# State space: GpSimd's waits on itself, projections in eighths, one output bank, four banks for the gated unit, idle products

## The chip, the cores and the metric

The kernel runs on one core of a Trainium2 chip, as one launch. The time is device time of that core in microseconds. Before the change it is 1918.82 us, the median of 3 runs (1918.71 to 1918.95). All arithmetic is in float32.

## The reference

Four transformer-like layers run over 256 tokens of width 1024: two layers of attention with a long convolution, an even layer (two kinds of attention, then a dense feed-forward), and an odd layer: a diagonal state space mixer, then a mixture of 8 experts, 2 per token. The change lies in the odd layer's mixer and in the router behind it, with one line ahead of the mixer's norm.

```python
def s5_mixer(h, w_in, lam_re, lam_im, log_dt, b_re, b_im, c_re, c_im, d_skip, w_glu, w_o):
    ...
    u = h @ w_in
    ug = u.reshape(B, S, S5_GROUPS, S5_GROUP)
    ...
    bu_re = jnp.einsum('sbgk,gpk->sbgp', ut, bb_re)
    bu_im = jnp.einsum('sbgk,gpk->sbgp', ut, bb_im)
    ...
    _, _, xr, xi = lax.associative_scan(combine, (ar_t, ai_t, bu_re, bu_im), axis=0)
    y = jnp.einsum('sbgp,gkp->bsgk', xr, c_re) - jnp.einsum('sbgp,gkp->bsgk', xi, c_im)
    y = y.reshape(B, S, D_MODEL) + d_skip * u
    y = jax.nn.gelu(y)
    y = y * jax.nn.sigmoid(y @ w_glu)
    return y @ w_o

def moe_swiglu(h, w_router, w_gate, w_up, w_down):
    logits = (h @ w_router).astype(jnp.float32)
    top_val, top_idx = lax.top_k(logits, TOP_K)
    weights = jax.nn.softmax(top_val, axis=-1)
    ...
```

There are 64 groups of 16 channels with 64 complex states each. The recurrence of a state over 256 tokens is computed as a rotation, a real scan with a decay, and a rotation back.

## The kernel before, in words

Every engine has a program of its own, written out by hand, and they meet through semaphores. TensorE writes to eight PSUM banks of 128 x 512 numbers. A float32 product is two matrix instructions in the trace.

**Projection.** `s5_in(c, j, part)` computes u = h @ w_in, transposed, in four chunks c of two blocks j of 128 channels. A part is four of the eight products that one block takes; the chunks use bank 2 and bank 3 in turn. ScalarE's `s5_in(c)` (L1554) copies a chunk to `uT` and counts `free`. Six parts run ahead of the state space (all of chunk 0 and half of chunk 1), the other ten one per round, by `IN_AT`.

**State tiles.** A state tile i (of 32) holds 128 states, those of two groups. Work goes in rounds p of two tiles:
- TensorE's `s5_state(p)` (L1103) multiplies `uT` by the input matrices into banks 4 and 5 or 0 and 1. It waits until VectorE is done with the pair of two rounds ago.
- VectorE rotates (L2243 to L2246) and scans (L2250, L2251) a tile, with each operation waiting for the one before, and counts `z5_ready`. The scan's result `zz` has two buffers, so tile i waits for `cz_ready` of tile i - 2.
- GpSimd rotates back: two products of 128 x 256 into `cz` (L2444), a difference (L2446) and a sum (L2447) into `xs`, which has four buffers. `link` makes GpSimd wait for each operation before it issues the next. It counts `cz_ready` once per tile.
- TensorE's `s5_out(o)` (L1119, L1122, L1126) multiplies the states of tiles o and o + 1 by the output matrices, two rounds behind the state products. Four tiles fill one output tile y in bank 6 or 7, in turn.
- VectorE's `y_tile(j)` (L2233) adds d_skip * u to an output tile, in program order behind state tile 4j + 6; ScalarE's `s5_gelu(j)` (L1559) follows.

**Gated unit.** `s5_glu(k, half)` (L1083) multiplies output tile k by four of the eight column blocks of w_glu, so 8 matrix instructions. The first half (banks 2 and 3) goes into rounds 10 to 15, the second (banks 4 and 5) into rounds 16 and 17, by `GLU_AT`. Round 17 holds eight such calls behind the last outputs. ScalarE then takes the sigmoid of a bank (L1571), VectorE multiplies (L2261), and TensorE multiplies by w_o (L1148).

**Weights.** SyncE requests six blocks of 2 MB into `wmix` (L444): blocks 0 and 1 for the projection, 2 and 3 for the gated unit once chunks 1 and 3 are projected (`grp_ps`), 4 and 5 for w_o behind tiles 8 and 24 (`cz_ready`). The experts' first weights are requested when the gated unit ends and when the output projection ends.

**Router.** Behind the norm, TensorE computes the logits (L1158, 16 products of 8 columns), waits for VectorE's choice of experts (`rt_step`), computes ranks (L1164 to L1168), waits for VectorE (`oh_ready`), gathers the first expert's tokens (L1029), loads the number of work items into a register, and starts the experts (L932, L950).

## Time and profile before

| | us |
|---|---|
| median of 3 runs | 1918.82 |
| the profiled execution | 1918.2 |
| its span | 1916.4 |
| TensorE busy | 1862.4 (97%) |
| VectorE busy | 644.5 (34%) |
| ScalarE busy | 357.7 (19%) |
| GpSimd busy | 113.3 (6%) |

The shares are averages over stages with different limits. The state space is the stretch from 1005 to 1122 us of the span, the output projection follows until 1149, norm and router until 1173, and the experts take the rest. Times in the rows below are us from the start of the span. A row of a timeline merges instructions of one line that follow each other: start, time until the last one's end, engine, line, operation, buffers, shapes and count. In brackets stands how long the engine was idle ahead of it, and what ended that.

### The profile page before, as it was taken

Reading aid. Unit: us, or ns where it says so; the run is one execution under the profiler, and the core shown is the slowest. Engines: PE = TensorE matmul, PEld = TensorE weight load, DVE = VectorE, ACT = ScalarE, POOL = GpSimd, SP = SyncE. Lnnn points to the kernel's source line nnn. Section 1 sums busy time; section 2 is a strip of 40 time slices with the busy share of each in tenths; the row PEclk is TensorE's granted clock in tenths of the full one; section 3 lists DMA queues with packets and bytes.
Section 4 is the critical chain, followed back from the end, with each engine's and each line's share of the span. In section 5 each row is a group of like instructions: output and inputs, shape, how many; then the busy total and the mean of one; then the engine's idle time right before and its main releaser. Section 6 shows DMA issues by size and latency. Waiting matters only on the chain.

```text
span 1916.4 us, 28949 instructions
## 1 busy us (share of the span) xinstructions
PE 1862.4 (97%) x12112; PEld 1040.3 (54%) x12112; DVE 644.5 (34%) x1479; ACT 357.7 (19%) x779; POOL 113.3 (6%) x166
## 2 busy tenths in 40 slices
PE   8999999999999999999998898999999999999998
PEld 6577866678775765867767664232323333333332
DVE  3464414354513484352357824010101010110102
ACT  3322103322103132233221012010101010101001
POOL 0000000000000000000006800000000000000000
PEclk9999999999999999999999998999999999999999
DMA  8345675254665314634421337999999999999993
GB/s 350 116 183 201 238 302 228 88 220 176 243 269 227 132 45 155 263 132 181 171 88 45 133 132 302 399 401 380 390 388 385 395 385 391 387 392 361 418 376 136
DMA packets 45529, 488.87 MB, mean 255 GB/s; under 512 B 5285, under 2 KB 6949, under 8 KB 11945
## 3 DMA queue, kind: packets, MB, share of 16 engines
q1 hardware_dynamic: 39136, 471.73, 61.6%
q10 hardware_dynamic: 5160, 11.82, 1.6%
q0 software_dynamic: 1152, 4.19, 0.6%
q8 instruction: 57, 0.93, 0.2%
q14 instruction: 24, 0.19, 0.0%
HBM read 481.82 MB, written 12.20 MB: 258 GB/s over the span
## 4 chain that ended last, share of the span: by engine, by line
PE 89%; DVE 4%; POOL 3%; issue 1%; ACT 1%; ACTq 1%; DMA 0%; DVEq 0%; POOLq 0%
PE bank L950 21%; PE bank L590 15%; PE bank L980 12%; PE bank L902 8%; PE bank L914 4%; PE bank L748 3%; PE bank L582 3%; PE bank L754 3%; PE bank L575 3%; POOL arena L2444 2%; PE bank L603 2%; PE bank L1148 1%; PE bank L571 1%; PE bank L964 1%; PE bank L1083 1%
## 5 line engine op out<-in xcount | busy, mean ns | idle before, releaser
L950 PE MATMUL bank<-arena 128*32 128x512 f32 x4096 | 457.5, 592 | 1.1 <-issue 1.1
L590 PE MATMUL bank<-arena 128*128 128x256 f32 x1408 | 313.3, 382 | 0.0
L950 PEld LDWEIGHTS bank<-arena 128*32 128x32 f32 x4096 | 136.7, 110 | 301.5 <-issue 301.5
L590 PEld LDWEIGHTS bank<-arena 128*128 128x128 f32 x1408 | 265.6, 191 | 53.0 <-issue 14.6
L980 PE MATMUL bank<-arena 128*32 128x512 f32 x2112 | 238.2, 595 | 0.0
L2195 DVE TENSOR_TENSOR arena<-arena,bank 128x256 f32<-128x256 f32 x64 | 27.0, 421 | 568.0 <-ACT arena L1521 517.8
L902 PE MATMUL bank<-arena 128*128 128x256 f32 x704 | 153.8, 379 | 0.1
L902 PEld LDWEIGHTS bank<-arena 128*128 128x128 f32 x704 | 133.2, 190 | 19.9 <-issue 2.1
L980 PEld LDWEIGHTS bank<-arena 128*32 128x32 f32 x2112 | 62.9, 109 | 133.8 <-issue 133.8
L1521 ACT ACTIVATE arena<-bank 128x256 f32<-128x256 f32 x64 | 24.6, 384 | 519.4 <-PE bank L950 519.3
L914 PE MATMUL bank<-arena 128*128 128x512 f32 x176 | 77.2, 592 | 0.0
L2444 POOL TENSOR_TENSOR arena<-arena 128x256 f32<-128x256 f32 x64 | 46.5, 727 | 258.0 <-DVE arena L2251 253.1
L575 PE MATMUL bank<-arena 128*128 128x512 f32 x128 | 55.4, 593 | 1.8 <-ACT arena L1215 1.8
L748 PE MATMUL bank<-arena 128*128 128x256 f32 x256 | 57.0, 381 | 0.0
L754 PE MATMUL bank<-arena 128*128 128x512 f32 x128 | 56.4, 596 | 0.2 <-DVE arena L2045 0.2
L582 PE MATMUL bank<-arena 128*128 128x256 f32 x256 | 56.3, 381 | 0.0
L914 PEld LDWEIGHTS bank<-arena 128*128 128x128 f32 x176 | 33.4, 190 | 37.8 <-issue 37.3
L582 PEld LDWEIGHTS bank<-arena 128*128 128x128 f32 x256 | 48.3, 190 | 9.8 <-issue 3.4
L748 PEld LDWEIGHTS bank<-arena 128*128 128x128 f32 x256 | 48.2, 190 | 7.5 <-issue 0.8
L2163 DVE TENSOR_TENSOR arena<-arena,bank 128x256 f32<-128x256 f32 x22 | 9.2, 421 | 125.4 <-ACT arena L1494 125.4
L2432 POOL TENSOR_TENSOR arena<-arena 128x512 f32<-128x512 f32 x22 | 28.1, 1279 | 363.9 <-ACT arena L1215 363.8
L603 PE MATMUL bank<-arena 128*32 128x512 f32 x384 | 45.8, 598 | 0.0
(472 smaller groups left out, 1741.5 us busy)
## 6 DMA issues: line engine op xcount, KB each, us to landing
arena<-in_wgu SPq DMA_DIRECT2D x88, 2048.0 KB, 10.8
arena<-in_w SPq DMA_DIRECT2D x46, 2048.0 KB, 8.2
arena<-in_wdn SPq DMA_DIRECT2D x88, 1024.0 KB, 11.1
arena<-in_modw SPq DMA_DIRECT2D x24, 2048.0 KB, 9.7
arena<-in_wf SPq DMA_DIRECT2D x11, 3072.0 KB, 10.2
arena<-slot_rows ACTq DMA_DIRECT2D x7, 384.0 KB, 11.3
arena<-in_flt_deltas ACTq DMA_DIRECT2D x2, 1024.0 KB, 11.6
slot_rows<-arena ACTq DMA_DIRECT2D x7, 192.0 KB, 6.3
```

Of the source, the lines that this page charges most:

```text
L575: ins = mm(bank[b][:, :], mT[:, k, h * P:(h + 1) * P], w[:, k * 512:(k + 1) * 512], start=(k == 0), stop=(k == KT - 1))
L582: ins = mm(bank[b][:, j * S:(j + 1) * S], w[:, col:col + P], y_in[:, k, :], start=(k == 0), stop=(k == 3))
L590: ins = mm(bank[b][:, j * S:(j + 1) * S], w[:, col:col + P], hT[:, k, :], start=(k == 0), stop=(k == KT - 1))
L603: ins = mm(bank[n % 2][r, :], band[:, k, 31 - c:63 - c], ring[at % RING][:, k * 512:(k + 1) * 512], start=(k < 4), stop=(k >= 4), skip_gro ...
L748: ins = mm(bank[n % 2][:, j * S:(j + 1) * S], w[:, col:col + P], hT[:, k, :], start=(k == 0), stop=(k == KT - 1))
L754: ins = mm(bank[n % 2][:, :], lhs(k), w[:, k * 512:(k + 1) * 512], start=(k == 0), stop=(k == KT - 1))
L902: ins = mm(bank[4 + f][:, u * S:(u + 1) * S], w[:, col:col + P], hT[:, k, :], start=(k == 0), stop=(k == KT - 1))
L914: ins = mm(bank[2 * t + i][:, :], hid[:, d % 2, f, t * P:t * P + P], w[:, col:col + 512], start=(d == 0 and f == 0), stop=(d == FFC - 1 an ...
L950: ins = mm(bank[w % 2][32 * j:32 * j + 32, :], hTe[:, k, TOK * b:TOK * b + TOK], wslot[SLOT[c]][:, k, :], start=(k == 0), stop=(k == KT - ...
L980: return mm(bank[4 + n][32 * g:32 * g + 32, :], lhs, dslot[c % RING][:, f, n * 512:(n + 1) * 512], start=first, stop=last, skip_group_chec ...
L2432: ins = pool.tensor_tensor(modsum, modsum, modout[:, n % 2, :], ALU.add)
L2444: link(pool.tensor_tensor(cz[:, n], zz[:, o % 2], tab[o][:, n, :].unsqueeze(1).broadcast_to([P, 2, PAIRS]), ALU.mult))
```

## The change

- **GpSimd:** within a tile only the difference waits, for both products (`link.mark` counts without waiting). `cz` has two buffers. `cz_ready` counts twice per tile, and every wait on it is doubled.
- **Projection:** a unit is two products (an eighth of a block pair's 16). Only chunk 0 runs ahead of the state space, the other 24 units go by `IN_STEPS` into rounds 0 to 10. All chunks use bank 2, so a chunk's first unit waits for ScalarE's copy of the chunk before.
- **Outputs:** all output tiles use bank 6. VectorE's `y_tile(j)` moves ahead by one state tile, and `s5_out` of a new output tile waits for it.
- **Gated unit:** `s5_glu(k, c)` does two of the eight column blocks (4 matrix instructions); the four groups have banks 3, 7, 2 and 5. Three of them go on during the state space.
- **ScalarE:** its first three gelus are issued between the copies.
- **Idle products:** `keep_warm(n, b)` multiplies the identity by 512 columns of constants into bank b, n times, and nobody reads it: one ahead of the norm before the mixer, two behind the logits, one ahead of the gather, three behind it.

On GpSimd, this is a state tile from the middle, before:

```order
L2444 TENSOR_TENSOR arena<-arena 128x256 [waits sy_ps,z5_ready,cz_ready]
L2444 TENSOR_TENSOR arena<-arena 128x256 [waits pool_chain]
L2446 TENSOR_TENSOR arena<-arena 128x128 [waits pool_chain]
L2447 TENSOR_TENSOR arena<-arena 128x128 [waits pool_chain]
L2444 TENSOR_TENSOR arena<-arena 128x256 [waits sy_ps,z5_ready,cz_ready]
L2444 TENSOR_TENSOR arena<-arena 128x256 [waits pool_chain]
```

And after, where L2471, L2473 and L2474 are the same operations:

```order
L2471 TENSOR_TENSOR arena<-arena 128x256 [waits cz_ready,sy_ps,z5_ready]
L2471 TENSOR_TENSOR arena<-arena 128x256
L2473 TENSOR_TENSOR arena<-arena 128x128 [waits pool_chain]
L2474 TENSOR_TENSOR arena<-arena 128x128
L2471 TENSOR_TENSOR arena<-arena 128x256 [waits cz_ready,sy_ps,z5_ready]
L2471 TENSOR_TENSOR arena<-arena 128x256
```

Two of the three waits inside a tile are gone. The wait for `cz_ready` that opens a tile asked for the tile just before, and now asks for the tile two back.

On TensorE, at the start of the state space, before (L1066 projection, L1103 state products; the first row is the rest of the products ahead of the loop):

```order
L1066 MATMUL bank<-arena 128x256 x16
L1103 MATMUL bank<-arena 128x128 [waits even_free]
L1103 MATMUL bank<-arena 128x128 x7
L1066 MATMUL bank<-arena 128x256 x4
L1103 MATMUL bank<-arena 128x128 x8
L1066 MATMUL bank<-arena 128x256 x4
```

And after (L1084 projection, L1122 state products):

```order
L1084 MATMUL bank<-arena 128x256 x8
L1122 MATMUL bank<-arena 128x128 [waits even_free]
L1122 MATMUL bank<-arena 128x128 x7
L1084 MATMUL bank<-arena 128x256 [waits even_free]
L1084 MATMUL bank<-arena 128x256 x5
L1122 MATMUL bank<-arena 128x128 x8
L1084 MATMUL bank<-arena 128x256 x6
```

Eight products moved from ahead of the first state products to behind them.

On TensorE, in the router, after (L1177 logits, L738 the idle products, L1184 to L1188 ranks, L1042 gather, L394 the register load); before, the rows are the same without those of L738:

```order
L1177 MATMUL bank<-ev,arena 128x8 x8
L738 MATMUL bank<-cst 128x512 x2
L1184 MATMUL bank<-arena,cst 128x8 [waits rt_step]
L1185 MATMUL bank<-arena,cst 128x8
L1186 MATMUL bank<-arena,cst 128x8
L1187 MATMUL bank<-arena,cst 128x8
L1188 MATMUL bank<-arena,cst 128x8
L738 MATMUL bank<-cst 128x512
L1042 MATMUL bank<-arena 128x96 [waits oh_ready,gb_ready]
L1042 MATMUL bank<-arena 128x96 x15
L738 MATMUL bank<-cst 128x512 x3
L394 TENSOR_LOAD itab [waits items_ready,hta_ready]
```

Each idle product stands ahead of a wait in TensorE's queue, and none waits itself.

```diff
--- before.py
+++ after.py
-IN_AT = {n: (1 + (n + 2) // 4, (n + 2) // 2 % 2, n % 2) for n in range(10)}
-GLU_AT = {**{10 + k: [(k, 0)] for k in range(6)}, 16: [(0, 1), (1, 1)], 17: [(6, 0), (2, 1), (3, 1), (4, 1), (7, 0), (5, 1), (6, 1), (7, 1)]}
+IN_UNITS = [(c, j, u) for c in range(1, 4) for j in range(2) for u in range(4)]
+IN_STEPS = [3, 3, 2, 3, 3, 1, 2, 1, 2, 1, 3]
+GLU_AT = {5: [(0, 0), (0, 1)], 7: [(1, 0), (1, 1)], 9: [(2, 0), (2, 1)], 11: [(3, 0), (3, 1)], 12: [(0, 2), (1, 2), (2, 2)],
+          13: [(4, 0), (4, 1)], 14: [(3, 2), (4, 2)], 15: [(5, 0), (5, 1)], 16: [(5, 2), (0, 3), (1, 3)],
+          17: [(6, 0), (6, 1), (6, 2)] + [(k, 3) for k in range(2, 7)] + [(7, c) for c in range(4)]}
+GLU_BANK = (3, 7, 2, 5)
...
-        cz = view(CH * 3 + 2048, 2, 2, PAIRS)
+        cz = [view(CH * 3 + at, 2, 2, PAIRS) for at in (2048, 512)]
...
-                    sp.wait_ge(sm["cz_ready"], (8, 24)[n - 4])
+                    sp.wait_ge(sm["cz_ready"], (16, 48)[n - 4])
...
+            def keep_warm(n, b):
+                for _ in range(n):
+                    mm(bank[b][:, :], ident, cst[:, 0:512], start=True, stop=True)
...
             gate_rows(3, gdiag5)
+            keep_warm(1, 4)
             norm(4, (0, 1, 4, 5))
-            def s5_in(c, j, part):
-                if j + part == 0 and c % 2 == 0:
-                    pe.wait_ge(landeds[c // 2], 16)
+            def s5_in(c, j, unit):
+                if j + unit == 0:
+                    if c % 2 == 0:
+                        pe.wait_ge(landeds[c // 2], 16)
+                    if c:
+                        n = G3 + c - 1
+                        pe.wait_ge(free[n % 2], n // 2 + 1)
                 w = wmix[c // 2]
-                for k in range(4 * part, 4 * part + 4):
+                for k in range(2 * unit, 2 * unit + 2):
...
-                    ins = mm(bank[2 + c % 2][:, j * S:(j + 1) * S], w[:, col:col + P], hT[:, k, :],
+                    ins = mm(bank[2][:, j * S:(j + 1) * S], w[:, col:col + P], hT[:, k, :],
...
-            def s5_glu(k, half):
+            def s5_glu(k, c):
                 if k == 0:
-                    if half:
+                    if c == 2:
+                        pe.wait_ge(free[(G3 + 3) % 2], (G3 + 3) // 2 + 1)
+                    elif c == 3:
                         pe.wait_ge(sm["z5_ready"], STATE_TILES - 2)
...
                 pe.wait_ge(sm["gelu_ready"], k + 1)
-                for o in range(4 * half, 4 * half + 4):
+                for o in (2 * c, 2 * c + 1):
...
-            for c, j, part in ((0, 0, 0), (0, 0, 1), (0, 1, 0), (0, 1, 1), (1, 0, 0), (1, 0, 1)):
-                s5_in(c, j, part)
+            for j in range(2):
+                for u in range(4):
+                    s5_in(0, j, u)
...
-                pe.wait_ge(sm["cz_ready"], o + 2)
-                if o % 4 == 0 and o >= 8:
-                    pe.wait_ge(sm["y_out"], j - 1)
+                pe.wait_ge(sm["cz_ready"], 2 * (o + 2))
+                if o % 4 == 0 and o:
+                    pe.wait_ge(sm["y_out"], j)
...
-                y = bank[6 + j % 2]
+                y = bank[6]
...
-                if p in IN_AT:
-                    s5_in(*IN_AT[p])
-                for k, half in GLU_AT.get(p, []):
-                    s5_glu(k, half)
+                for unit in IN_UNITS[sum(IN_STEPS[:p]):sum(IN_STEPS[:p + 1])]:
+                    s5_in(*unit)
+                for k, c in GLU_AT.get(p, []):
+                    s5_glu(k, c)
...
+            keep_warm(2, 3)
             pe.wait_ge(sm["rt_step"], 1)
...
+            keep_warm(1, 3)
             pe.wait_ge(sm["gb_ready"], 4)
             gather()
+            keep_warm(3, 3)
             pe.wait_ge(sm["hta_ready"], 28)
...
             s5_in(0)
             s5_in(1)
+            s5_gelu(0)
             s5_in(2)
-            s5_gelu(0)
+            s5_gelu(1)
+            s5_gelu(2)
             s5_in(3)
-            for j in range(1, 8):
+            for j in range(3, 8):
                 s5_gelu(j)
...
-                        dve.wait_ge(sm["cz_ready"], i - 1)
+                        dve.wait_ge(sm["cz_ready"], 2 * (i - 1))
...
-                if i >= 6 and i % 4 == 2:
+                if i >= 5 and i % 4 == 1:
                     y_tile(i // 4 - 1)
...
+                if o >= 2:
+                    pool.wait_ge(sm["cz_ready"], 2 * o - 2)
+                t = cz[o % 2]
                 for n in range(2):
-                    link(pool.tensor_tensor(cz[:, n], zz[:, o % 2],
-                                            tab[o][:, n, :].unsqueeze(1).broadcast_to([P, 2, PAIRS]), ALU.mult))
-                link(pool.tensor_tensor(xs[o % 4][:, 0, :], cz[:, 0, 0, :], cz[:, 1, 1, :], ALU.subtract))
-                pool.tensor_tensor(xs[o % 4][:, 1, :], cz[:, 0, 1, :], cz[:, 1, 0, :], ALU.add).then_inc(sm["cz_ready"], 1)
-                pool.wait_ge(sm["cz_ready"], o + 1)
+                    (link if n else link.mark)(pool.tensor_tensor(t[:, n], zz[:, o % 2],
+                                                                  tab[o][:, n, :].unsqueeze(1).broadcast_to([P, 2, PAIRS]), ALU.mult))
+                pool.tensor_tensor(xs[o % 4][:, 0, :], t[:, 0, 0, :], t[:, 1, 1, :], ALU.subtract).then_inc(sm["cz_ready"], 1)
+                pool.tensor_tensor(xs[o % 4][:, 1, :], t[:, 0, 1, :], t[:, 1, 0, :], ALU.add).then_inc(sm["cz_ready"], 1)
```

## Rows read from the trace of the kernel before

**Rows 1.** the chain that ended last, 995 to 1210 us, shares by line

```profile
by line: POOL arena L2444 18.5%; PE bank L950 12.9%; PE bank L1148 12.8%; PE bank L1083 8.8%; PE bank L1066 6.3%; POOL arena L2447 6.0%; POOL arena L2446 5.7%; issue 4.5%; PE bank L1029 2.9%; PE bank L980 2.1%; PE bank L1158 1.6%; PE bank L
```

**Rows 2.** groups of instructions on GpSimd; count, busy us, mean ns, idle before

```profile
L2444 POOL TENSOR_TENSOR arena<-arena 128x256 f32<-128x256 f32 x64 | 46.5, 727 | 258.0 <-DVE arena L2251 253.1
...
L2446 POOL TENSOR_TENSOR arena<-arena 128x128 f32<-128x128 f32 x32 | 14.5, 454 | 2.5
```

**Rows 3.** timeline, GpSimd, first and last state tile; start us, us

```profile
1019.34 1.54 POOL L2444 TENSOR_TENSOR arena<-arena 128x256 f32<-128x256 f32 x2 [253.07 <-DVE arena L2251]
...
1102.27 1.53 POOL L2444 TENSOR_TENSOR arena<-arena 128x256 f32<-128x256 f32 x2
```

**Rows 4.** timeline, VectorE, first operation of state tiles 0, 1, 6 and 7

```profile
1016.79 0.42 DVE L2243 TENSOR_TENSOR arena<-bank,arena 128x256 f32<-128x256 f32 x1 [10.62 <-PE bank L1103]
...
1019.29 0.42 DVE L2243 TENSOR_TENSOR arena<-bank,arena 128x256 f32<-128x256 f32 x1
...
1031.74 0.42 DVE L2243 TENSOR_TENSOR arena<-bank,arena 128x256 f32<-128x256 f32 x1
...
1034.63 0.42 DVE L2243 TENSOR_TENSOR arena<-bank,arena 128x256 f32<-128x256 f32 x1
```

**Rows 5.** timeline, TensorE, round 10 and the start of round 11

```profile
1065.40 1.18 PE L1103 MATMUL bank<-arena 32*128 32x128 f32 x16
...
1067.48 0.41 PE L1119 MATMUL bank<-arena 32*32 32x128 f32 x4 [0.91 <-POOL arena L2447]
...
1070.74 1.18 PE L1103 MATMUL bank<-arena 32*128 32x128 f32 x16
```

**Rows 6.** timeline, TensorE, from round 16 on

```profile
1101.20 5.07 PE L1083 MATMUL bank<-arena 128*128 128x256 f32 x16
...
1106.21 0.41 PE L1119 MATMUL bank<-arena 32*32 32x128 f32 x4
...
1107.55 14.08 PE L1083 MATMUL bank<-arena 128*128 128x256 f32 x64
```

**Rows 7.** timeline, start of the state space: first copy, first state products

```profile
1012.15 0.60 ACT L1554 ACTIVATE arena<-bank 128x512 f32<-128x512 f32 x1 [4.61 <-PE bank L1066]
...
1015.49 1.18 PE L1103 MATMUL bank<-arena 32*128 32x128 f32 x16
```

**Rows 8.** timeline, GpSimd, two memsets at the start

```profile
0.28 0.12 POOL L2605 MEMSET const-bfloat16-1.0<- 128x1 bf16 x1
...
0.31 0.12 POOL L2605 MEMSET const-uint8-127<- 128x1 uint8 x1
```

**Rows 9.** transfers into wmix, 990 to 1100 us, time to landing

```profile
DMA to landing us min/median/max: 7.8/8.0/12.7
```

**Rows 10.** timeline, TensorE, gate rows and the transposes of the next norm

```profile
998.48 1.88 PE L734 MATMUL bank<-arena,cst 128*128 128x512 f32 x4
...
1002.16 1.09 PE L519 MATMUL bank<-cst,arena 128*128 128x128 f32 x8 [1.80 <-DVE arena L1611]
```

**Rows 11.** windows: us, busy (count) of PE, PEld, DVE, ACT, POOL, clock, DMA share, GB/s

```profile
1161.00:1165.00 4.00, 2.65 (x13) 2.58 (x13) 2.38 (x11) 0.00 (x0) 0.00 (x0) 0.50 1.01 428
...
1200.00:1300.00 100.00, 99.71 (x906) 30.81 (x898) 10.82 (x23) 9.81 (x22) 0.00 (x0) 1.00 0.98 395
```

**Rows 12.** timeline, norm and router

```profile
1151.76 1.97 PE L519 MATMUL bank<-cst,arena 128*128 128x128 f32 x16 [0.85 <-DVE arena L1611]
...
1153.71 3.98 PE L1158 MATMUL bank<-ev,arena 128*128 128x8 f32 x32
...
1159.85 0.60 PE L1164 MATMUL bank<-arena,cst 128*128 128x8 f32 x2 [2.17 <-DVE arena L2359]
...
1162.27 0.18 DVE L2368 SCALAR_TENSOR_TENSOR arena<-bank,arena 128x16 f32<-128x16 f32 x1 [2.07 <-PE bank L1168]
...
1163.51 6.32 PE L1029 MATMUL bank<-arena 128*128 128x96 f32 x32 [1.35 <-DVE arena L2281]
...
1172.69 3.37 PE L932 MATMUL bank<-arena 128*32 128x512 f32 x16 [2.86 <-issue]
```

19 lines of the change are left out of this document (10 added, 9 removed).

## The prediction

> **What bounds the kernel now.** I read the chain that ended last first. Between 995 and 1210 us it lies mostly on GpSimd: L2444, L2446 and L2447 hold 30% of that stretch [rows 1]. Next I read GpSimd's groups: four operations per state tile, two of 727 ns and two of 454 ns (L2447 like L2446), 2.36 us of work [rows 2]. The timeline gives the cadence: tile 0 starts at 1019.34 and tile 31 at 1102.27, so 2.675 us per tile [rows 3]. The difference, 0.314 us, is four gaps of 0.078 us, one ahead of each operation, because each waits for the one before it. So GpSimd is never starved, and the state space costs 32 of its periods.
>
> VectorE is the next limit. One of its tiles takes 2.49 us (1019.29 to 1031.74 is five), and 2.89 us where an output tile is added, which makes 0.40 us for that [rows 4]. Four tiles cost it 4 x 2.49 + 0.40 = 10.36 us, against GpSimd's 10.70.
>
> TensorE comes third. From one pair of tiles to the next it has 5.34 us, of which it waits 0.91 us for GpSimd [rows 5]. After GpSimd's last tile, however, TensorE alone has the path: output products, 64 instructions of the gated unit, and then L1148 [rows 6].
>
> **Part 1: the start.** Before, 48 projection instructions run ahead of the first state products, though the first chunk of 32 is enough for them. ScalarE copies that chunk at 1012.15 in 0.60 us, while the state products start only at 1015.49 [rows 7]. After, TensorE stops at the chunk and waits for the copy: 1012.15 + 0.60 + 0.10 for the hand-over = 1012.85. Gain 2.64 us; VectorE's first tile moves from 1016.79 [rows 4] to 1014.15. The idle time of TensorE ahead of the copy, some 0.8 us, is already in this sum. The second chunk now comes in 3 + 3 + 2 units between pairs. It is wanted in round 4, so nothing waits for it.
>
> **Part 2: the loop.** Three of GpSimd's four waits on itself go (only the subtraction keeps one). Operations of GpSimd that do not wait are shown once, the memsets at the start: of 0.12 us each, they start 0.03 us apart, so they overlap by 0.09 us [rows 8]. Bounds of the new cadence, then: 2.675 us if the gaps are not due to the waits; 2.36 + 0.078 = 2.44 if they close; 2.675 - 3 x (0.078 + 0.09) = 2.17 if the operations also overlap. I take 2.44, the sum of the tensor rows themselves. The choice hardly matters, because VectorE at 10.36 per four tiles is slower than 9.76 and takes over the pace. VectorE runs 32 x 2.49 + 7 x 0.40 = 82.5 us, so its last scan ends at 1014.15 + 82.5 = 1096.65, and GpSimd's last tile 0.09 + 2.44 later, at 1099.2. Before it was 1102.27 + 2.59 = 1104.86. That is 5.7 us earlier: 2.6 from the start, 3.1 from the loop.
>
> On the pages: the Trainium skill, GPSIMD Engine Reference, section 2.1 (Instruction dispatch), says that a Pool instruction does not hold the next one back, and that each of its cores goes on as soon as its own share is done. The memsets agree with it [rows 8]. By that rule the 2.17 would stand; the sum stays the same.
>
> Is the cover there? Between pairs TensorE has 4.43 us of work with 8 instructions of projection or gated unit (5.34 - 0.91). One instruction of these costs 14.08 / 64 = 0.22 us [rows 5, 6]. The new tables put 2 or 3 units of 4 instructions into each round, 36 over rounds 3 to 16, 2.57 on average: 4.43 + 0.57 x 0.88 = 4.93 us, under VectorE's 5.18 per pair. A round with three units takes 5.31, over it by 0.13; state products are made a pair ahead, so this is absorbed.
>
> The output tiles now share one bank, and VectorE adds tile j - 1 one state tile earlier, behind state tile 4j + 1. TensorE's last outputs for it wait for GpSimd's tile 4j - 1, which with GpSimd in step ends 2.5 us after VectorE starts state tile 4j, and take 1.4 (L1119 to the last L1126), so they end at 3.9; the addition comes at 2 x 2.49 = 4.98. It has 1.1 us to spare. TensorE wants the bank again 2.4 us after the addition. Neither waits. The one projection bank costs a wait for a ScalarE copy (0.6 plus two hand-overs) in round 6, which has two units only. On SyncE, the weights of units (k, 2) are requested when the projections end, in round 10, and are wanted about 7.6 us later; such a transfer lands after 7.8 to 12.7 us [rows 9], the longest being the second of two issued together. The weights for the output projection, queued behind it, are not wanted before the loop ends. This is 0.2 us late if it lands like the fastest, 5 if like the slowest. I take 0.2, since it is the first of its two, and state products a pair ahead hide some 2 us.
>
> **Part 3: behind the loop.** Before, the last output products started at 1106.21, not at 1104.9, because 16 gated-unit instructions took 5.07 us (0.32 each instead of 0.22) [rows 6]. After, round 16 holds 12 instructions, 2.6 us at full clock and 4 at the slower pace. They start behind outputs at about 1094.2 + 1.34, so they end at 1098.2 to 1099.7. I take the later: 0.5 us late instead of 1.35, a gain of 0.8. Behind the last outputs there stood 64 instructions, now 48 (12 units of 4): 16 x 0.22 = 3.5 us less. The sigmoids of the first three groups end before the last unit does, as the last four units are one per group, 0.88 us apart, and a sigmoid takes no longer than the 0.60 of the copy of that shape in [rows 7]. Parts 1 to 3 sum to 2.6 + 3.1 + 0.8 + 3.5 = 10.0 us.
>
> **Part 4: idle products.** One is two instructions; the four at L734 take 1.88 us, so a product costs 0.86 to 0.94 at full clock [rows 10]. The one ahead of the norm ends near 1001.2, and TensorE waited 1.80 us there, until 1002.16: cost and gain nothing. It is hidden by VectorE's norm; without that cover it would cost its 0.9.
>
> At the router the clock had fallen to 1.2 GHz (granted 0.50) [rows 11] behind an idle time of 2.17 us. There ten small instructions run from 1159.85 until VectorE answers at 1162.27, and then 32 gather instructions take 6.32 us [rows 12]. The same small kind cost 3.98 / 32 = 0.124 each just before, and transposes of 128 columns 1.97 / 16 = 0.123. Warm, the ten take 1.3 instead of 2.3 us (gain 1.0) and the gather 32 x 0.123 = 3.9 instead of 6.3 (gain 2.4). The two products in the 2.17 us end before the wait does, the one ahead of the gather lies beside 1.24 us of VectorE. The three behind the gather take 2.6 to 2.8 us, where 2.86 passed anyway before the experts' first products. These three are what can cost: if the register load for the loop begins only behind them, up to 1.1 us is lost. Those first products, 16 in 3.37 us, would take 1.7 warm, by half (gain 1.65). Together 3.9 to 5.1; I take 3.9. Behind it TensorE is busy 99.7 of 100 us [rows 11] and every weight load waits for it, so the shift is kept.
>
> **Sum.** 10.0 + 3.9 = 13.9 us. The profiled execution took 1918.2 (span 1916.4), 0.6 under the median; from it 1904.3, from the median 1904.9. Small waits of the fuller TensorE are likelier than further gains, so I say 1905.2.
>
> **Rivals.**
> (a) GpSimd's gaps are no waits on itself: cadence 2.675 remains and the loop's 3.1 is not had. 1918.8 - 10.8 = 1908.0. The even 0.078 gaps behind every dependent step speak for it, the memsets against. Chance 0.12.
> (b) The clock is not held at the router: products at half speed last 3.5 us and overrun their 2.17 by 1.3, one before the gather as much again. The gather turns warm somewhere, the experts' first products are warm. Router gain 0.3 instead of 3.9: 1908.7. For it: the clock fell soon after the small products, so they may have weighed little. Chance 0.18.
> (c) TensorE becomes the bound: its reserve is 0.25 us per pair by my sum, and every wait for a copy, for weights or for the shared output bank eats from it. With all 16 pairs at 5.31 the loop loses 2.1, with a full late transfer 3 more: 1907.3 to 1910. Chance 0.17. The Trainium skill, Perfetto Trace Analysis, section Matmul Optimizations, asks for all eight PSUM banks to be in use; the change takes banks from projection and outputs. The trace of before has no wait for such a bank, so no run here yet shows the rule at work.
> (d) Slower: VectorE and GpSimd, now closer packed, slow each other in SBUF. From 0.43 us more per VectorE tile (17%) the gain is gone (32 x 0.43 = 13.8); with a quarter more on its 2.3 us busy, 0.57, it ends at 1904.9 + 18.2 = 1923. Against it: VectorE's first tile, with GpSimd idle, took 2.50 us, the later ones 2.49 [rows 4]. Chance 0.03.
> Forecast itself: 0.50.
>
> **Range.** The cases (a) to (c) reach from 1907 to 1910, all warm with overlap to 1902.5. So 1902 to 1910.5. What a measurement of this kernel can tell from no change is 0.2%, 3.8 us: faster means under 1915.0. All but (d), and mixtures of (a), (b) and (c) that go further than priced, lie there: faster 0.93, within 0.04, slower 0.03.
>
> **What would show it.** First state products at 1012.9 and VectorE's first tile at 1014.2; GpSimd's tiles spaced 2.49 with 2.89 once in four, and waiting for VectorE; its last one ending at 1099; 48 gated-unit instructions behind the last outputs in 10.5 us; L1148's successor at 1111.5. At the router granted clock 1.00, gather 3.9 us. Wrong would be: GpSimd without idle time at 2.67, VectorE waiting for TensorE inside the loop, or TensorE at 0.50 in the router.

## The result and the profile after

The changed kernel takes 1907.13 us, the median of 4 runs (1906.01 to 1908.76), against 1918.88 for the kernel before in the same comparison. The ratio is 0.9942, with a 95% interval of 0.9930 to 0.9953, so it is faster by 0.6%. The forecast was 1905.2 us, the range 1902.0 to 1910.5. The profiled execution took 1906.32 us (span 1904.5) against 1918.2 (1916.4).

A table of four landmarks shows where the 11.9 us came from. All are starts, in us of the span; the experts' second wave is the first L950 (after: L963).

| | gated addition ahead of the mixer | projection by w_o | logits | experts' second wave | last projection |
|---|---|---|---|---|---|
| before | 995.35 | 1121.47 | 1153.71 | 1175.88 | 1905.88 |
| after | 994.75 | 1110.34 | 1142.59 | 1160.72 | 1893.98 |
| stage before | | 126.12 | 32.24 | 22.17 | 730.00 |
| stage after | | 115.59 | 32.25 | 18.13 | 733.26 |
| difference | -0.60 | -10.53 | +0.01 | -4.04 | **+3.26** |

The -0.60 is not the change's: over all kernels run here this first landmark lies between 994.1 and 995.9, in no order. The state space and the router gave 14.6 us, close to the 13.9 forecast. The experts, whose code is the same, gave 3.26 back. The idle product ahead of the norm cost nothing and gained nothing, as forecast: from the gated addition to the first transposes (L519, after: L527) it is 6.81 us in both kernels.

**The start**, on the timelines of ScalarE, TensorE and VectorE, answers to [rows 4, 7]:

```profile
1011.57 0.60 ACT L1576 ACTIVATE arena<-bank 128x512 f32<-128x512 f32 x1 [4.60 <-PE bank L1084]
...
1012.22 1.18 PE L1122 MATMUL bank<-arena 32*128 32x128 f32 x16 [0.69 <-ACT arena L1576]
...
1013.51 0.42 DVE L2267 TENSOR_TENSOR arena<-bank,arena 128x256 f32<-128x256 f32 x1 [7.92 <-PE bank L1122]
```

The state products start as soon as the copy is done (1011.57 + 0.60), and VectorE's first tile 1.3 us behind them.

**The loop.** First GpSimd, a whole tile and its last (answers to [rows 3]), then VectorE around an output tile:

```profile
1018.54 1.41 POOL L2471 TENSOR_TENSOR arena<-arena 128x256 f32<-128x256 f32 x2
1020.03 0.46 POOL L2473 TENSOR_TENSOR arena<-arena 128x128 f32<-128x128 f32 x1
1020.44 0.46 POOL L2474 TENSOR_TENSOR arena<-arena 128x128 f32<-128x128 f32 x1
1021.03 1.41 POOL L2471 TENSOR_TENSOR arena<-arena 128x256 f32<-128x256 f32 x2
...
1098.03 0.45 POOL L2474 TENSOR_TENSOR arena<-arena 128x128 f32<-128x128 f32 x1
```

```profile
1025.97 0.42 DVE L2267 TENSOR_TENSOR arena<-bank,arena 128x256 f32<-128x256 f32 x1
1028.46 0.48 DVE L2257 SCALAR_TENSOR_TENSOR arena<-arena,ev,bank 128x256 f32<-128x256 f32 x1
1028.86 0.42 DVE L2267 TENSOR_TENSOR arena<-bank,arena 128x256 f32<-128x256 f32 x1
1031.34 0.42 DVE L2267 TENSOR_TENSOR arena<-bank,arena 128x256 f32<-128x256 f32 x1
```

GpSimd's tiles are now 2.49 us apart, as VectorE's are. The two products last 1.41 us together (before 1.54), though one alone takes 0.73, and the sum starts 0.41 us behind the difference although that one is shown with 0.46: operations that do not wait overlap by about 0.05 us here. VectorE waits for nobody between its first and its last tile.

**The tail**, on TensorE (L1101 gated unit, L1138 the first rows of an output), answers to [rows 6]:

```profile
1094.40 2.86 PE L1101 MATMUL bank<-arena 128*128 128x256 f32 x12
1098.54 0.42 PE L1138 MATMUL bank<-arena 32*32 32x128 f32 x4 [1.27 <-POOL arena L2474]
...
1099.88 10.63 PE L1101 MATMUL bank<-arena 128*128 128x256 f32 x48
```

**The router**, on TensorE, and three windows over it (columns as in [rows 11]), answer to [rows 12]:

```profile
1142.59 3.98 PE L1177 MATMUL bank<-ev,arena 128*128 128x8 f32 x32
1146.42 3.62 PE L738 MATMUL bank<-cst 128*128 128x512 f32 x4
1149.83 0.36 PE L1184 MATMUL bank<-arena,cst 128*128 128x8 f32 x2
...
1152.45 3.78 PE L1042 MATMUL bank<-arena 128*128 128x96 f32 x32 [0.40 <-DVE arena L2305]
1156.07 2.77 PE L738 MATMUL bank<-cst 128*128 128x512 f32 x6
1158.99 1.92 PE L945 MATMUL bank<-arena 128*32 128x512 f32 x16 [0.15 <-issue]
```

```profile
1142.00:1146.00 4.00, 3.94 (x35) 3.62 (x33) 2.16 (x5) 3.75 (x7) 0.00 (x0) 1.00 1.02 434
1146.00:1150.00 4.00, 4.00 (x12) 1.94 (x11) 2.14 (x9) 1.17 (x3) 0.00 (x0) 0.57 0.96 412
1150.00:1154.00 4.00, 3.60 (x27) 2.81 (x26) 2.42 (x11) 0.00 (x0) 0.00 (x0) 1.00 1.01 422
```

The granted clock falls to its lower level just as the first two idle products start; they take 3.62 us instead of 1.9, and the ranks (L1184) start 1.15 us after VectorE has produced their input (1148.68). Behind them the clock is full: the gather takes 3.78 us instead of 6.32. The wait of 2.86 us before the experts' first products has shrunk to 0.15, so the register load ran beside the last three idle products (2.77 us) and not behind them.

**The experts.** The loss lies in one place, TensorE's exit from the loop over the work items into the straight code of the last ones (L945 opens an item, before: L932). From the second wave to this exit the two kernels take 637.21 and 637.25 us, from the exit to the last projection 92.79 and 96.01. First the rows of before, then those of after, then the clock there:

```profile
1813.09 1.90 PE L932 MATMUL bank<-arena 128*32 128x512 f32 x16
1814.80 1.03 PE L950 MATMUL bank<-arena 128*32 128x512 f32 x5
1816.90 6.63 PE L950 MATMUL bank<-arena 128*32 128x512 f32 x58 [1.07 <-issue]
```

```profile
1797.97 1.03 PE L945 MATMUL bank<-arena 128*32 128x512 f32 x6
1801.59 2.41 PE L945 MATMUL bank<-arena 128*32 128x512 f32 x9 [2.59 <-issue]
```

```profile
1800.00:1802.00 2.00, 0.41 (x4) 0.15 (x7) 1.90 (x4) 0.00 (x0) 0.00 (x0) 0.98 1.02 422
1802.00:1804.00 2.00, 2.00 (x16) 0.75 (x12) 1.34 (x4) 0.00 (x0) 0.00 (x0) 0.50 1.01 422
1804.00:1806.00 2.00, 2.00 (x19) 0.64 (x15) 0.00 (x0) 0.60 (x1) 0.00 (x0) 0.66 1.03 422
```

"issue" means that the profile shows no semaphore and no transfer of data that held the engine. Before, it stood still for 1.07 us after 21 matrix instructions of the straight code; after, for 2.59 us after 6, and ran at the lower clock for more than 2 us behind that.

### The profile page after: what moved, and what is told of

It reads as the page before. It is cut to its first block, busy times and chain, and to the rows that moved or that the text cites. A ratio compares the mean times of both kernels' runs of the same rounds, so it can differ in the third digit from the quotient of the medians.

```text
span 1904.5 us, 28978 instructions
## 1 busy us (share of the span) xinstructions
PE 1863.0 (98%) x12126; PEld 1037.8 (54%) x12126; DVE 644.4 (34%) x1479; ACT 359.0 (19%) x779; POOL 110.8 (6%) x166
## 4 chain that ended last, share of the span: by engine, by line
PE 87%; DVE 7%; DMA 2%; issue 1%; ACT 1%; ACTq 1%; POOL 0%; DVEq 0%
PE bank L963 21%; PE bank L598 14%; PE bank L993 12%; PE bank L915 8%; PE bank L927 4%; PE bank L761 3%; PE bank L590 3%; PE bank L767 3%; PE bank L583 3%; PE bank L611 2%; PE bank L1167 1%; PE bank L579 1%; DMA arena<-bias_rows 1%; PE bank L977 1%; PE bank L692 1%
## 5 line engine op out<-in xcount | busy, mean ns | idle before, releaser
L963 PE MATMUL bank<-arena 128*32 128x512 f32 x4096 | 458.4, 593 | 0.0
L963 PEld LDWEIGHTS bank<-arena 128*32 128x32 f32 x4096 | 137.7, 110 | 299.4 <-issue 299.4
L598 PEld LDWEIGHTS bank<-arena 128*128 128x128 f32 x1408 | 265.2, 190 | 52.9 <-issue 14.6
L2471 POOL TENSOR_TENSOR arena<-arena 128x256 f32<-128x256 f32 x64 | 45.3, 729 | 257.3 <-DVE arena L2275 254.3
```

The costliest lines, as they stand in the source:

```text
L598: ins = mm(bank[b][:, j * S:(j + 1) * S], w[:, col:col + P], hT[:, k, :], start=(k == 0), stop=(k == KT - 1))
L963: ins = mm(bank[w % 2][32 * j:32 * j + 32, :], hTe[:, k, TOK * b:TOK * b + TOK], wslot[SLOT[c]][:, k, :], start=(k == 0), stop=(k == KT - ...
L2471: (link if n else link.mark)(pool.tensor_tensor(t[:, n], zz[:, o % 2], tab[o][:, n, :].unsqueeze(1).broadcast_to([P, 2, PAIRS]), ALU.mult))
```

## The experiments

The theory at this point: the standstill sits at a fixed place of TensorE's instruction stream. The changed kernel has 7 idle products, 14 matrix instructions, more ahead of it, so the place comes 14 or 15 instructions sooner behind the exit (measured, 21 - 6, it is 15; the fifteenth is not accounted for). The rival: the standstill has to do with the experts' data, their weights or their timing. Other experiments take single parts of the change back. "Padding" below is a number N of idle products of 8 columns (two matrix instructions each) in the even layer, at 762 us, so far ahead of all that is measured here:

```diff
             gate_rows(2)
+            for _ in range(N):
+                mm(bank[5][:, 0:8], ident, cst[:, 0:8], start=True, stop=True)
```

**1. The kernel before with padding, N = 7.**

> The kernel before, with 7 products of 8 columns (14 matrix instructions) put into TensorE's idle time ahead of the norm before the dense feed-forward, nobody reads them. Theory (place in the program): TensorE's standstill behind the experts' loop, 1.07 us in the kernel before and 2.59 in the changed one, sits at a fixed place of the instruction stream; the changed kernel has 14 matrix instructions more ahead of it, so the standstill comes 15 instructions earlier behind the loop's end and less of it is covered. Then these 14 alone give the kernel before a standstill of about 2.6 us and, if the clock falls behind it, some 2 us more: 1920.4 to 1922. Rival (the standstill depends on when the transfers run): it stays at 1.1 us, 1918.9.

Measured: 1921.21 us (1918.95 to 1924.4), ratio 1.0014 with an interval of 1.0005 to 1.0024. The exit on TensorE:

```profile
1815.19 1.03 PE L932 MATMUL bank<-arena 128*32 128x512 f32 x7
1818.96 1.45 PE L932 MATMUL bank<-arena 128*32 128x512 f32 x9 [2.73 <-issue]
```

The longer standstill of the changed kernel appears in the kernel before, 7 matrix instructions behind the exit instead of 21. From the exit to the last projection it now takes 94.46 us instead of 92.79. That is 1.67 us, and only this part is the standstill's. The profiled execution was 3.78 us longer than that of before; another 1.25 lie in the router and 1.31 at the start of the experts, where the lower clock lasted longer (granted 0.50 until 1179; before, 0.84 in 1175 to 1177 and then 1.00). So the whole time met the expectation for more reasons than the expected one, and the rows of the exit are the evidence.

**2. The changed kernel with padding, N = 4.**

> The changed kernel with 4 such products of 8 columns (8 matrix instructions) at the same place. In the changed kernel the standstill comes 6 instructions of the first kind behind the loop's end. Place in the program: moved by 8 it falls into the loop's body, where the stream is already running, and the standstill goes: experts from their first product to the last in 730 us or less instead of 733, and 1903 to 1904.5 in all; or it appears at the next such place with more cover. Rival: nothing changes, 1907.

Measured: 1901.78 us (1901.29 to 1902.13), ratio 0.9915 (0.9899 to 0.9932). The exit has no standstill:

```profile
1797.45 1.90 PE L945 MATMUL bank<-arena 128*32 128x512 f32 x16
1799.16 7.05 PE L963 MATMUL bank<-arena 128*32 128x512 f32 x64
```

The experts' stage takes 728.73 us, 4.53 less than in the changed kernel. This kernel beats both, and is faster than expected by 1.2 us or more, in part because its router took 1.04 us less too (experiment 8).

**3. The changed kernel with N = 8, N = 2 and N = 6, and the kernel before with N = 12.**

> Eight products of 8 columns (16 matmuls) behind the second gate rows, where the kernel with four such products came to 1901.78 us. Theory (TensorE's standstill on leaving the expert loop sits at a fixed place of its instruction stream, 6 matmuls behind the loop in the changed kernel; with 8 more matmuls ahead it lies in front of the loop's exit and is not met there): with 16 it stays away too; the added products cost about 0.06 us each where they stand, so 1901.5 to 1902.8 us. Rival (the standstill comes back at every so many instructions, and four products only happened to miss it): a standstill of 1 to 3 us again within some dozens of TensorE instructions behind the exit, and 1903 to 1905.

> Two products of 8 columns (4 matmuls) behind the second gate rows. Theory (fixed place in TensorE's stream; without padding the standstill came 6 matmuls behind the expert loop, with 8 and 16 more it was not met): it comes 2 matmuls behind the loop, 2.6 us long, with the clock at 0.50 behind it as in the changed kernel: from the first expert product to the last projection 735 us (it was 735.0 without padding and 730.5 with four and eight products), time 1905.5 to 1907.5. Rival (any padding realigns the code and takes it away): 730.5 us there, and 1901.3 to 1903.5.

> Six products of 8 columns (12 matmuls) and all idle products; beside the same padding without the first two idle products (1903.27 us). No standstill at the exit (730.5 us from the first expert product to the last projection). Theory A (whether the clock falls at the end of the logits goes by the whole work ahead, and the two products behind them neither hold it nor bring it back before the pairs): anywhere between the router of four and of eight such products, 15.4 to 17.4 us from the first logits product to the first expert product, 1901.3 to 1903.7. Theory B (the two products are worth a steady 2.5 us at the pairs): 15.4 us there, 1901.2 to 1901.9.

> The kernel before, with twelve products of 8 columns (24 matmuls) behind the second gate rows. In the kernel before the standstill of 1.07 us comes 21 matmuls behind the expert loop; with 14 matmuls ahead it came after 7 and lasted 2.73. Theory (fixed place): with 24 it lies in front of the exit and is not met: no idle time of TensorE over 0.5 us within 100 matmuls behind the exit, 0.7 to 1.1 us shorter from the first expert wave to the last projection than the 730.0 us of before; time 1917.5 to 1918.8 with the cost of the padding. Rival (there is always one standstill behind the exit, wherever it falls): 1 to 2.8 us of it again, 1919.5 or more.

Measured: 1903.68 us for N = 8 (ratio 0.9906 to 0.9939), 1908.12 for N = 2 (0.9930 to 0.9963), 1902.03 for N = 6 (0.9902 to 0.9935), and 1918.36 for the kernel before with N = 12 (0.9992 to 1.0011). For N = 6 and for the kernel before the times lie where the theory (for N = 6, theory A) had them; the stage of the latter is 1.23 us shorter than in the kernel before, expected were 0.7 to 1.1. The other two missed: N = 8 has no standstill, but came out in the range of its rival, because its router took 19.12 us (experiment 8), and N = 2 has the standstill where it was expected, but not the lower clock behind it (granted 1.00 from 1802 to 1810), and came out above its range because its router took 22.42 us. The exit with N = 2, with the place where the theory put it:

```profile
1802.03 1.02 PE L945 MATMUL bank<-arena 128*32 128x512 f32 x2
1805.65 1.49 PE L945 MATMUL bank<-arena 128*32 128x512 f32 x11 [2.60 <-issue]
```

The page lists a transfer queue of the kind "instruction". Asked in steps of 0.2 us, it shows one packet of some 16 KB (57 packets hold 0.93 MB) at every exit; this is its row in the changed kernel, in 1799.00 to 1799.20 (packets, MB, share of 16 engines in the window):

```profile
q8 instruction: 1, 0.02, 31.8%
```

| | matrix instructions from exit to standstill | exit | packet, from | goes on | idle, us | exit to last projection, us | experts' stage, us |
|---|---|---|---|---|---|---|---|
| before | 21 | 1813.09 | 1814.5 | 1816.90 | 1.07 | 92.79 | 730.00 |
| before, N = 7 | 7 | 1815.19 | 1816.5 | 1818.96 | 2.73 | 94.46 | 732.98 |
| before, N = 12 | none | 1813.47 | 1815.3 | | 0 | 91.53 | 728.77 |
| after | 6 | 1797.97 | 1799.0 | 1801.59 | 2.59 | 96.01 | 733.26 |
| after, experiment 4 | 6 | 1803.08 | 1804.2 | 1806.70 | 2.59 | 96.01 | 733.24 |
| after, experiment 5 | 6 | 1804.10 | 1805.4 | 1807.72 | 2.59 | 96.01 | 733.26 |
| after, experiment 6 | 6 | 1804.01 | 1805.0 | 1807.36 | 2.31 | 95.75 | 732.98 |
| after, N = 2 | 2 | 1802.03 | 1803.3 | 1805.65 | 2.60 | 94.33 | 731.57 |
| after, no router products (7 below) | 18 | 1802.12 | 1803.4 | 1805.94 | 1.08 | 92.81 | 730.02 |
| after, N = 4 | none | 1797.45 | 1798.6 | | 0 | 91.52 | 728.73 |
| after, N = 6 | none | 1798.09 | 1799.4 | | 0 | 91.53 | 728.78 |
| after, N = 8 | none | 1800.11 | 1801.4 | | 0 | 91.53 | 728.78 |

The place moves by one for each matrix instruction added ahead: 21 - 14 = 7, and 6 - 4 = 2; without 12 of them it is 6 + 12 = 18. Experiments 4 to 6 leave the number of instructions ahead as it is, and the place stays at 6. Where the sum falls below zero (6 - 8, 21 - 24), nothing stands still, and the stage takes the same 728.8 us in four kernels. So the standstill belongs to a place in TensorE's stream, and not to the experts' data or their timing.

What happens at the place is a reading. The packet starts 1.0 to 1.8 us after the exit in every kernel, and TensorE goes on 2.3 to 2.6 us after the packet's start, so 3.35 to 3.82 us after the exit. This fits a block of code that is fetched only when the loop has been left: an engine that reaches the block's border earlier waits for it, and one whose next border lies farther behind does not. That the packet belongs to TensorE is inferred from this agreement of times; the trace doesn't name its engine.

**4. The changed kernel, with GpSimd waiting on itself again.** `cz` keeps its two buffers.

```diff
-                    (link if n else link.mark)(pool.tensor_tensor(...))
+                    link(pool.tensor_tensor(...))
                 ...subtract).then_inc(sm["cz_ready"], 1)
+                pool.wait_ge(sm["cz_ready"], 2 * o + 1)
                 ...add).then_inc(sm["cz_ready"], 1)
+                pool.wait_ge(sm["cz_ready"], 2 * o + 2)
```

> The changed kernel with GpSimd waiting for itself behind each of its four operations again; all else as changed. Theory (the waits set GpSimd's cadence, VectorE the new one): GpSimd's tiles are 2.675 us apart instead of 2.59 on average, it has no idle time in the loop, and its last tile ends about 3 us later: 1910.1 if the rest is unchanged. Rival (the waits were worth nothing and the gain comes from the start and from what stands behind the loop): as the changed kernel, 1907.

Measured: 1911.13 us (1909.79 to 1914.07), ratio 0.9965 (0.9952 to 0.9977), 4.0 more than the changed kernel. A tile of GpSimd:

```profile
1018.59 1.53 POOL L2471 TENSOR_TENSOR arena<-arena 128x256 f32<-128x256 f32 x2
1020.20 0.46 POOL L2473 TENSOR_TENSOR arena<-arena 128x128 f32<-128x128 f32 x1
1020.73 0.45 POOL L2475 TENSOR_TENSOR arena<-arena 128x128 f32<-128x128 f32 x1
1021.26 1.54 POOL L2471 TENSOR_TENSOR arena<-arena 128x256 f32<-128x256 f32 x2
```

The cadence is 2.67 us again, and the even gaps are back. GpSimd ends 3.24 us later, counted from the gated addition, where the forecast had 3.1 for this part. The gated projection begins 3.65 us later; the other 0.4 is TensorE's, which idled for 2.03 us, then took 4.49 us for the 12 instructions of round 16 (changed kernel 2.86) at a granted clock of 0.51, and so came 0.46 us late to the last outputs instead of 0.06.

**5. The changed kernel with half of chunk 1 ahead of the loop again.**

```diff
-IN_STEPS = [3, 3, 2, 3, 3, 1, 2, 1, 2, 1, 3]
+IN_STEPS = [2, 2, 0, 3, 3, 1, 2, 1, 2, 1, 3]
...
+            for unit in IN_UNITS[:4]:
+                s5_in(*unit)
...
-                for unit in IN_UNITS[sum(IN_STEPS[:p]):sum(IN_STEPS[:p + 1])]:
+                for unit in IN_UNITS[4:][sum(IN_STEPS[:p]):sum(IN_STEPS[:p + 1])]:
```

> The changed kernel, with the first half of the second chunk's input projection (4 units, 16 matmuls) ahead of the recurrence again, and the rounds 0 to 2 lighter by as much. Theory (the place of these units is what brought the first tile forward by 2.7 us, and the recurrence is the pace from there on): first tile on VectorE 2.2 to 3.5 us later than 1013.5, gated projection begins 2.2 to 3.5 us later than 1110.3, time 1908.5 to 1910.5. Rival (the start is given back in the loop, where TensorE has to make up the work): gated projection at 1110.3 to 1111, time 1906 to 1907.5.

Measured: 1913.5 us (1911.63 to 1916.15), ratio 0.9974 (0.9964 to 0.9984). The stage up to the gated projection is 4.94 us longer. Of this, 3.65 is VectorE's first tile. That is more than the 2.68 that the change gained there, mostly since both chunks use bank 2 now and chunk 1 first waits 0.69 us for ScalarE's copy, which it did not in the kernel before. Another 1.24 is what VectorE waits inside the loop, where the changed kernel has no such wait (timeline of VectorE), and the cause is on TensorE:

```profile
1043.10 0.48 DVE L2259 SCALAR_TENSOR_TENSOR arena<-arena,ev,bank 128x256 f32<-128x256 f32 x1 [1.00 <-PE bank L1147]
...
1053.66 0.48 DVE L2259 SCALAR_TENSOR_TENSOR arena<-arena,ev,bank 128x256 f32<-128x256 f32 x1 [0.24 <-PE bank L1147]
```

```profile
1026.71 2.08 PE L1124 MATMUL bank<-arena 32*128 32x128 f32 x16 [1.05 <-DVE arena L2277]
...
1031.56 3.71 PE L1084 MATMUL bank<-arena 128*128 128x256 f32 x12
```

Rounds 0 to 2 are light now, TensorE idles in them, and then runs at half pace: the granted clock is 0.81, 0.50 and 0.84 in the three windows of 4 us from 1024 on, where the changed kernel has 1.00; 16 state products take 2.08 us instead of 1.18, and 12 projection instructions 3.71 instead of 2.86.

**6. The changed kernel with four gated-unit calls moved behind the last outputs.**

```diff
-          13: [(4, 0), (4, 1)], 14: [(3, 2), (4, 2)], 15: [(5, 0), (5, 1)], 16: [(5, 2), (0, 3), (1, 3)],
-          17: [(6, 0), (6, 1), (6, 2)] + [(k, 3) for k in range(2, 7)] + ...
+          13: [(4, 0), (4, 1)], 14: [(3, 2)], 15: [(5, 0), (5, 1)], 16: [],
+          17: [(6, 0), (6, 1), (4, 2), (5, 2), (6, 2)] + [(k, 3) for k in range(7)] + ...
```

> The changed kernel, with four of the gated unit's products (16 matmuls) taken out of rounds 14 and 16 and put behind the last output products, where 64 then run alone instead of 48. Theory (the tail behind the last tile is TensorE's alone, 0.22 us for each matmul): the run behind the last outputs lasts 14.1 instead of 10.6 us, the gated projection begins 3.5 us later, about 1113.8, time 1909.5 to 1910. Rival (TensorE was late at the last tiles because of those products, and comes to the last outputs earlier without them): less than 2 us, time under 1908.5.

Measured: 1915.42 us (1912.09 to 1916.98), ratio 0.9984 (0.9974 to 0.9993). The stage is 5.09 us longer, not 3.5:

```profile
1097.88 0.41 PE L1138 MATMUL bank<-arena 32*32 32x128 f32 x4 [4.06 <-POOL arena L2474]
1098.23 0.90 PE L1141 MATMUL bank<-arena 128*32 128x127 f32 x8
...
1099.91 15.02 PE L1101 MATMUL bank<-arena 128*128 128x256 f32 x64
```

Sixteen instructions at 0.22 us are the 3.5. The rest is the clock: TensorE idles for 4.06 us before the last outputs and begins the tail slowly (granted 0.61 in 1098 to 1100 and 0.54 in the 2 us behind; L1141 x8 in 0.90 us instead of 0.63, the 64 in 15.02 instead of the 14.08 of [rows 6]).

The stage is the measure of experiments 4 to 6, not the whole time. From the first logits product to the experts' second wave the three take 19.76, 19.77 and 19.76 us against 18.13 in the changed kernel, with the same code there; their logits last 5.06 to 5.40 us instead of 3.98. So 1.6 us of each whole time come from the router, and the expected times of experiments 5 and 6, 3.0 and 5.4 us too low at their upper ends, missed this as well as the clock in the stage. The profiled execution of experiment 6 is the fastest of ten (1912.09 us); why the median lies 3.3 us above it no trace shows.

**7. The changed kernel without the idle products at the router.** The three calls of `keep_warm` behind the logits are left out.

> The changed kernel without the six idle products at the router; the one ahead of the norm stays. Theory: the router from the logits' end to the experts' first wave takes 18.2 us as in the kernel before instead of 14.3, so 4 us are lost there. By the theory of the place in the program, 12 of the 14 matrix instructions go too, the standstill behind the experts' loop returns to some 1.3 us without a fall of the clock, and 3 us come back: 1907 to 1908 in all. Rival (the standstill has nothing to do with them): 1911.

Measured: 1907.6 us (1907.27 to 1907.98), ratio 0.9946 (0.9929 to 0.9962), hardly different from the changed kernel. But two effects nearly cancel, as was expected. Its router, up to the second wave, takes 22.39 us, 4.26 more, with [rows 12] back nearly to the letter:

```profile
1148.67 0.59 PE L1183 MATMUL bank<-arena,cst 128*128 128x8 f32 x2 [2.17 <-DVE arena L2380]
...
1152.33 6.49 PE L1042 MATMUL bank<-arena 128*128 128x96 f32 x32 [1.35 <-DVE arena L2302]
1161.56 3.52 PE L945 MATMUL bank<-arena 128*32 128x512 f32 x16 [2.74 <-issue]
```

Its experts take 730.02 us, 3.24 less, because with 12 instructions fewer ahead the place of the standstill lies farther behind the exit (1.08 us of standstill).

**8. The changed kernel with N = 6, without the first two idle products.**

> The changed kernel without the two idle products behind the logits (4 matmuls), and with six products of 8 columns (12 matmuls) behind the second gate rows, so that the exit from the expert loop has the same place in the stream as with four and all idle products (1901.78 us). Theory A (those two products hold the clock through the lone pairs and the gathered one-hot products): pairs at 0.57 us and the 32 products of 96 columns slow as in the kernel without idle products, first expert product 1.5 to 2.6 us later than 1158.5, time 1903.3 to 1904.5. Theory B (the clock falls at the end of the logits or not whatever these two do, and where it falls they only delay the pairs): the first expert product within 0.6 us of 1158.5, time 1901.2 to 1902.4.

Measured: 1903.27 us (1903.07 to 1903.88), against 1902.03 with them. Its router takes 20.23 us, against 18.12 in the same kernel with them. That is theory A, with the first expert product 2.56 us later than 1158.5 (expected 1.5 to 2.6). The other paddings show how far this is luck. From the first logits product to the experts' second wave:

| | no router products | without the first two, N = 6 | N = 0 | N = 2 | N = 4 | N = 6 | N = 8 |
|---|---|---|---|---|---|---|---|
| us | 22.39 | 20.23 | 18.13 | 22.42 | 17.09 | 18.12 | 19.12 |

The best is N = 4. Its window answers to the second one above, and the idle products fit the wait for VectorE:

```profile
1146.00:1150.00 4.00, 3.66 (x22) 2.35 (x21) 2.13 (x9) 1.42 (x2) 0.00 (x0) 1.00 1.03 434
```

```profile
1146.99 1.96 PE L738 MATMUL bank<-cst 128*128 128x512 f32 x4
1149.29 0.39 PE L1186 MATMUL bank<-arena,cst 128*128 128x8 f32 x2 [0.34 <-DVE arena L2385]
```

The worst, N = 2, gains nothing over having no idle products. There the clock fell already within the logits (granted 0.81 in 1144 to 1146, 0.50 from then until 1158), and the gather too ran slowly:

```profile
1142.37 4.86 PE L1179 MATMUL bank<-ev,arena 128*128 128x8 f32 x32
1147.08 3.76 PE L738 MATMUL bank<-cst 128*128 128x512 f32 x4
...
1154.47 5.82 PE L1042 MATMUL bank<-arena 128*128 128x96 f32 x32
```

So the two products were worth 2.1 us at N = 6, but where the clock falls and comes back is not set by them alone, and the stage differs by up to 5.3 us between kernels whose code is the same here. A steady worth of the two, as theory B of the run with N = 6 had it, is refuted: from the first logits product to the first expert product it took 16.39 us and not 15.4. What they are worth at another padding was not tried.

## Why the prediction was right and wrong

**Part 1, the start: right.** Forecast 2.64 us, measured 2.68 (VectorE's first tile 3.28 earlier, of which 0.60 came from ahead of the stage). Experiment 5 shows that the step also had a use that the forecast didn't price: with the work moved into the first rounds TensorE has the full clock there, and without it 0.50 to 0.84.

**Part 2, the loop: right.** GpSimd's waits on itself were the gaps, and VectorE took over the pace. GpSimd ends 5.78 us earlier, counted from the gated addition; the forecast was 5.7 for start and loop. Rival (a) fell with experiment 4, rival (c) with VectorE's timeline (it waits for nobody in the loop), and rival (d) with its tiles, which take 2.49 us as before. The copy of the single projection bank cost TensorE 0.69 us, and 0.78 us passed ahead of the units (k, 2), both inside its reserve. The profile puts these 0.78 down to "issue"; by their time they may be the wait for the weights, requested at 1066.47 and, at the usual 7.9 us, there at 1074.4, where TensorE goes on at 1074.54. Of the rule that the prediction took from the Trainium skill, GPSIMD Engine Reference, section 2.1 (a Pool instruction does not hold the next one back), the trace shows a part: the two products overlap by 0.05 us, and so do the last two operations. That is about half of the 0.09 that the bound of 2.17 assumed, and a tile is still 2.36 us from its start to the sum's end, since the difference waits for both products. Whether GpSimd alone would keep 2.44 us isn't shown, because VectorE sets the pace.

**Part 3, the tail: right, a little small.** From GpSimd's end to the gated projection it took 16.61 us before and 11.86 after, so 4.75 instead of 0.8 + 3.5 = 4.3. The remainder is the pace: round 16's instructions ran at full clock (2.86 us) and ended before GpSimd did, so the outputs began 0.06 us behind it and not 0.5. One-sided experiments overstate such parts: taken back singly, they cost 3.65, 4.94 and 5.09 us, together 13.7, while the stage had gained 10.5. Each one also lets TensorE idle and pays for the lower clock behind that (0.51, 0.50 to 0.84, 0.54 to 0.61), and experiment 5 pays for the shared bank. The single output bank, the four banks of the gated unit and the order of ScalarE's gelus were not taken back by themselves.

**Part 4, the router: right in sum by luck, wrong in two terms.** Forecast 3.9, which is 1.0 + 2.4 + 1.65 less the 1.1 of a register load that begins only behind the last three idle products; measured 4.04. The small products and the wait for VectorE's answer gave 1.04 (forecast 1.0), the gather and the wait behind it 2.64 (2.4), the experts' first wave 1.46 (1.65). The 1.1 for the register load did not come: the wait was 0.15 us. What failed is "the two products in the 2.17 us end before the wait does", a cost that the sum had at nothing: they ran at the lower clock and cost 1.10. The two errors cancel. Rival (b) had that price (1.3) and its cause right, but the rest of its picture wrong: behind them the clock was full. "TensorE at 0.50 in the router", a sign of being wrong, came true for these products. Experiment 8 shows that the gain is not one number: the stage takes 17.09 to 22.42 us with the same code, so against the 22.17 of before it lies between 5.1 and nothing.

**Behind the router: wrong.** The step that failed is "behind it TensorE is busy 99.7 of 100 us and every weight load waits for it, so the shift is kept". It rested on a window of 100 us in the loop; the exit from the loop, at 1813, was not looked at. There the added instructions moved the place of TensorE's standstill from 21 to 6 instructions behind the exit, and 3.26 us went. I had counted the idle products' time, and not that they shift everything behind them in the stream. Without that loss the profiled execution would be at 1903.1, near the 1904.3 of the forecast's terms, and 0.6 of the difference came from ahead of the stage. None of TensorE's waits in the loop reached the path, so the 0.9 us added for "small waits of the fuller TensorE" had nothing behind them. The measured 1907.13 lies in the range because the range left room for rivals (a) to (c); none of them happened as priced.

With the padding of four products the kernel takes 1901.78 us: 4.5 us come from the exit and 1.04 from a luckier router, less 0.6 for a later start of the stage.

## What to carry to other kernels

An instruction added anywhere moves every later one in its engine's stream. Where a loop is left, look at the first 4 us behind it for an idle time that the profile puts down to "issue", and see whether a few idle instructions ahead move it away: here four idle products, eight matrix instructions, were worth nearly half as much as the whole change (5.35 of 11.75 us, of which 4.5 at the exit). Idle products against a falling clock are worth trying where a wait of their length follows anyway, and are to be judged with several paddings ahead of them, since one kernel shows only one case: here 17.09 to 22.42 us for the same code. And spread the work over the rounds: where three light rounds let TensorE idle, the clock fell and the stage lost 1.3 us more than its start, which a count of instructions doesn't show.

## What the runs showed of the hardware

- Behind the exit from the loop over the work items, a packet of some 16 KB on an instruction queue starts 1.0 to 1.8 us later. TensorE stood still at a fixed place of its instruction stream until 3.35 to 3.82 us after the exit: for 1.07 us with 21 matrix instructions between exit and place, 1.08 with 18, 2.73 with 7, 2.31 to 2.59 with 6 (four kernels) and 2.60 with 2. With the place ahead of the exit it did not stand still (four kernels of the table).
- A standstill of 2.6 to 2.7 us cost 2.8 us from the exit to the last projection in one kernel (N = 2) and 2.9 in another (before, N = 7), and 4.5 in the changed one, since the granted clock behind it stayed at 1.00 (2.4 GHz) in the first two and fell to 0.50 (1.2 GHz) in the third. What decides between them stays open.
- The clock at the router falls within the logits (N = 2, experiments 4 to 6), within the idle products behind them (N = 0, 6, 8) or not at all (N = 4, granted 1.00 from 1142 to 1160), with the same code there. Why was not settled.
- Two idle products of 512 columns took 1.96 us where the clock was full (N = 4) and 3.62 and 3.76 where it was falling or had fallen (N = 0 and 2).
- GpSimd's operations that don't wait start before the earlier one has ended: two products of 128 x 256, 0.73 us each, take 1.41 us instead of 1.54, and the last two operations, 0.46 us each, start 0.41 us apart instead of 0.53.
